# Two edits to the small matmuls of a two-block transformer kernel: scores of both directions added before one product with the values; softmax attention heads taken in pairs on halves of the array

## The reference, cut to what matters

```
scores = einsum('bhnik,bhnjk->bhnij', qe, ke)
scores = jnp.where(mask, scores, 0.0)
o_intra = jnp.einsum('bhnij,bhnjv->bhniv', scores, v)
...
o_inter = jnp.einsum('bhnik,bhnkv->bhniv', q * jnp.exp(b), s_start)
o = (o_intra + o_inter)
...
o_l = o_l + _flip(ol_d, d, 2)
```

```
s = jnp.einsum('bnigrd,bnjgd->bgrnij', qb, kk).astype(f32) * (dh ** -0.5)
s = s - slopes[None, :, :, None, None, None] * dist.astype(f32)[None, None, None, None]
...
m = jnp.maximum(jnp.max(s, axis=-1, keepdims=True), sink)
p = jnp.exp(s - m)
p = p / (jnp.sum(p, axis=-1, keepdims=True) + jnp.exp(sink - m))
out = jnp.einsum('bgrnij,bnjgd->bnigrd', p, vv.astype(f32))
...
y_s = swa @ w_swa_out[l]
```

## Time and profile before

| | |
|---|---|
| median of 3 runs | 909.81 us (908.39 to 911.15) |
| the profiled execution | 909.08 us, of which its span is 907.3 us |
| TensorE busy | 892.5 us of the span |
| TensorE weight loads busy | 808.8 us |
| VectorE busy | 655.4 us |
| ScalarE busy | 492.6 us |
| mean traffic | 177 GB/s |

### The profile page before, as it was taken

The page is one execution under the profiler, slowest core; times in us unless marked ns, Lnnn a source line. Parts: engine busy times, 40 slices in busy tenths (PEclk is TensorE's granted clock), DMA queues, the critical chain, the costliest instruction groups (busy, mean ns, idle before and its releaser), DMA issues.

```text
span 907.3 us, 17399 instructions
## 1 busy us (share of the span) xinstructions
PE 892.5 (98%) x6478; PEld 808.8 (89%) x6478; DVE 655.4 (72%) x1092; ACT 492.6 (54%) x769; POOL 0.2 (0%) x4
## 2 busy tenths in 40 slices
PE   8999999999999999999999999999999999999997
PEld 3578888888899999999999998999998899999996
DVE  3977798888886777766678978876576765555555
ACT  4632576666674655555557444454464664444443
POOL 0000000000000000000000000000000000000000
PEclk9999999999999999999999999999999999999999
DMA  9758844444435355556554643355446366555551
GB/s 339 296 187 284 313 149 140 139 139 139 139 116 202 111 192 194 185 165 201 173 178 139 209 140 123 111 186 182 153 164 210 111 203 208 185 185 185 186 185 47
DMA packets 45583, 160.88 MB, mean 177 GB/s; under 512 B 5216, under 2 KB 6624, under 8 KB 45408
## 3 DMA queue, kind: packets, MB, share of 16 engines
q1 hardware_dynamic: 43488, 156.27, 50.5%
q10 hardware_dynamic: 2048, 3.97, 1.2%
HBM read 159.16 MB, written 1.05 MB: 177 GB/s over the span
## 4 chain that ended last, share of the span: by engine, by line
PE 88%; DVE 4%; DMA 3%; ACT 3%; issue 2%; SPq 0%; DVEq 0%; ACTq 0%
PE bank L429 21%; PE bank L431 21%; PE bank L430 21%; PE bank L495 4%; PE bank L496 4%; PE bank L497 4%; DMA arena<-in_ada 2%; DMA raw<-in_stream 1%; PE bank L1154 1%; DVE arena L1586 1%; ACT w_hi L416 1%; PE bank L1299 1%; PE bank L1279 1%; PE bank L1295 1%; PE bank L1197 1%
## 5 line engine op out<-in xcount | busy, mean ns | idle before, releaser
L423 DVE TENSOR_TENSOR w_lo<-raw,w_hi 128x1024 fp32r<-128x1024 f32 x252 | 304.4, 1223 | 136.0 <-ACT w_hi L416 135.6
L429 PE MATMUL bank<-h_hi,w_hi 128*128 128x256 f32 (+1 forms) x1232 | 369.2, 300 | 2.3 <-DVE w_lo L423 1.4
L430 PE MATMUL bank<-h_lo,w_hi 128*128 128x256 f32 (+1 forms) x1232 | 361.6, 293 | 0.0
L431 PE MATMUL bank<-h_hi,w_lo 128*128 128x256 f32 (+1 forms) x1232 | 361.2, 293 | 0.0
L416 ACT ACTIVATE w_hi<-raw 128x1024 fp32r<-128x1024 f32 x252 | 261.0, 1051 | 134.9 <-PE bank L431 87.5
L429 PEld LDWEIGHTS bank<-h_hi,w_hi 128*128 128x128 f32 x1232 | 231.2, 188 | 12.7 <-issue 2.9
L430 PEld LDWEIGHTS bank<-h_lo,w_hi 128*128 128x128 f32 x1232 | 232.1, 188 | 6.5
L431 PEld LDWEIGHTS bank<-h_hi,w_lo 128*128 128x128 f32 x1232 | 232.5, 189 | 5.9
L429 PE MATMUL bank<-y_hi,w_hi 128*128 128x256 f32 x304 | 86.9, 286 | 0.0
L430 PE MATMUL bank<-y_lo,w_hi 128*128 128x256 f32 x304 | 85.8, 282 | 0.0
L431 PE MATMUL bank<-y_hi,w_lo 128*128 128x256 f32 x304 | 85.3, 281 | 0.0
(11 more groups left out here) (255 smaller groups left out, 1095.1 us busy)
## 6 DMA issues: line engine op xcount, KB each, us to landing
raw<-in_stream SPq DMA_DIRECT2D x252, 512.0 KB, 4.2
arena<-in_ada SPq DMA_DIRECT2D x32, 512.0 KB, 5.1
xres<-in_ada SPq DMA_DIRECT2D x8, 512.0 KB, 3.3
tok<-in_tok SPq DMA_DIRECT2D x3, 512.0 KB, 9.5
con<-in_con ACTq DMA_DIRECT2D x1, 1472.0 KB, 11.2
xres<-in_tok ACTq DMA_DIRECT2D x1, 1024.0 KB, 8.3
out<-arena SPq DMA_DIRECT2D x4, 256.0 KB, 2.1
tok<-in_tok SPq DMA_DIRECT2D x2, 256.0 KB, 11.2
```

The costliest lines, as they stand in the source:

```text
L423: dve.tensor_tensor(w_lo[c.slot][:, :], raw[c.slot][:, :], w_hi[c.slot][:, :].bitcast(F32), ALU.subtract).then_inc(S("split_lo"), 1)
L429: pe.matmul(dst, hi_w, a_hi, start=start, stop=False, skip_group_check=True)
L430: pe.matmul(dst, hi_w, a_lo, start=False, stop=False, skip_group_check=True)
L431: return pe.matmul(dst, lo_w, a_hi, start=False, stop=stop, skip_group_check=True)
```

## The change

**Recurrence.** After the masked copy, DVE adds the two directions' halves of `sc_T` into a new 128 by 256 area `sc_both` (in `wide`), after waiting for its own masked copy. `outputs` waits for this addition, and multiplies `v_cur` with `sc_both` once for each block, instead of twice with `sc_T`.

**Softmax attention.** Step e now handles head `head_of(e)`: 0, 4, 1, 5, 2, 6, 3, 7. Slopes and sinks follow. The scores of steps e and e+1 (e even) are issued together behind tile 10 + 2e, one head on the lower and one on the upper 64 rows, in turn, into banks 5 and 6. The values of steps e-1 and e (e odd) are issued together behind tile 14 + 2e, one head on the lower and one on the upper 64 columns, in turn. DVE copies the results of both heads at once. The rows of `w_swa_out_2` are reordered on the host to match.

```diff
+def head_of(e):
+
+    return 4 * (e % 2) + e // 2
...
+        sc_both = wide[:, 3584:3584 + NB * P]
...
             def probs_copy(e):
                 act.wait_ge(S("p_turned"), e + 1)
                 if e >= 2:
-                    act.wait_ge(S("pv"), e - 1)
+                    act.wait_ge(S("pv"), e // 2)
...
-                pe.wait_ge(S("masked"), h + 1)
+                pe.wait_ge(S("masked"), h * 2 + 2)
                 pe.wait_ge(S("state"), h * 4 + 4)
                 for b in range(NB):
                     dst = o_bank[:, b * P:(b + 1) * P]
-                    for d in range(2):
-                        x = (2 * d + b) * P
-                        pe.matmul(dst, v_cur[:, b * P:b * P + P], sc_T[:, x:x + P], start=d == 0, stop=False,
-                                  skip_group_check=True)
+                    pe.matmul(dst, v_cur[:, b * P:b * P + P], sc_both[:, b * P:b * P + P], start=True, stop=False,
+                              skip_group_check=True)
...
             def swa_scores(e):
-                g, x = e // 4, (e % 4) * T
-                rows = slice(S_DH * g, S_DH * g + S_DH)
+                x = e // 2 * T
                 if e == 0:
                     pe.wait_ge(S("in2_copied"), T_VS)
-                if e >= 2:
-                    pe.wait_ge(S("s_biased"), e - 1)
-                dst = psum[5 + e % 2]
-                pe.matmul(dst[:, 0:P], s_q[rows, x:x + P], s_k[rows, 0:P], start=True, stop=True, skip_group_check=True)
-                pe.matmul(dst[:, P:3 * P], s_q[rows, x + P:x + T], s_k[rows, 0:T], start=True, stop=True,
-                          skip_group_check=True).then_inc(S("s_scores"), 1)
+                else:
+                    pe.wait_ge(S("s_biased"), e)
+                for g in range(2):
+                    rows = slice(S_DH * g, S_DH * g + S_DH)
+                    pe.matmul(psum[5 + g][:, 0:P], s_q[rows, x:x + P], s_k[rows, 0:P], start=True, stop=True,
+                              skip_group_check=True)
+                for g in range(2):
+                    rows = slice(S_DH * g, S_DH * g + S_DH)
+                    pe.matmul(psum[5 + g][:, P:3 * P], s_q[rows, x + P:x + T], s_k[rows, 0:T], start=True, stop=True,
+                              skip_group_check=True).then_inc(S("s_scores"), 1)
...
             def swa_values(e):
-                g, q = e // 4, S_DH * (e % 2)
+                pair = e // 2
                 pe.wait_ge(S("p_T"), e + 1)
-                if e == 0:
+                if pair == 0:
                     pe.wait_ge(S("v2"), 1)
-                if e >= 2:
-                    pe.wait_ge(S("swa"), e - 1)
-                pe.matmul(psum[4][q:q + S_DH, 0:T], s_v[:, S_DH * g:S_DH * g + S_DH], s_pT[e % 2][:, 0:T],
-                          start=True, stop=False, skip_group_check=True)
-                pe.matmul(psum[4][q:q + S_DH, P:T], s_v[:, P + S_DH * g:P + S_DH * g + S_DH], s_pT[e % 2][:, T:3 * P],
-                          start=False, stop=True, skip_group_check=True).then_inc(S("pv"), 1)
+                else:
+                    pe.wait_ge(S("swa"), pair)
+                for g in range(2):
+                    q = S_DH * g
+                    pe.matmul(psum[4][q:q + S_DH, 0:T], s_v[:, q:q + S_DH], s_pT[g][:, 0:T], start=True, stop=False,
+                              skip_group_check=True)
+                for g in range(2):
+                    q = S_DH * g
+                    last = pe.matmul(psum[4][q:q + S_DH, P:T], s_v[:, P + q:P + q + S_DH], s_pT[g][:, T:3 * P], start=False,
+                                     stop=True, skip_group_check=True)
+                last.then_inc(S("pv"), 1)
...
-                for after, step in ((0, swa_scores), (3, turn_probs), (4, swa_values)):
-                    if swa_at(t, after) is not None:
-                        step(swa_at(t, after))
+                if swa_at(t, 0) is not None and swa_at(t, 0) % 2 == 0:
+                    swa_scores(swa_at(t, 0))
+                if swa_at(t, 3) is not None:
+                    turn_probs(swa_at(t, 3))
+                if swa_at(t, 4) is not None and swa_at(t, 4) % 2 == 1:
+                    swa_values(swa_at(t, 4))
...
+                dve.wait_ge(S("masked"), h * 2 + 1)
+                dve.tensor_tensor(sc_both, sc_T[:, 0:NB * P], sc_T[:, NB * P:], ALU.add).then_inc(S("masked"), 1)
...
             def swa_copy(e):
-                q = S_DH * (e % 2)
-                dve.wait_ge(S("pv"), e + 1)
-                dve.tensor_copy(swa[q:q + S_DH, (e // 2) * T:(e // 2 + 1) * T], psum[4][q:q + S_DH, 0:T]).then_inc(S("swa"), 1)
+                pair = e // 2
+                dve.wait_ge(S("pv"), pair + 1)
+                dve.tensor_copy(swa[:, pair * T:(pair + 1) * T], psum[4][:, 0:T]).then_inc(S("swa"), 1)
...
+    swa_out = a["w_swa_out_2"][0].reshape(2, 4, S_DH, D).transpose(1, 0, 2, 3).reshape(512, D)
```

More of the change, by code:

```diff
@@ L1014, in softmax_exp @@
             def softmax_exp(e):
-                p = e % 2
+                p, head = e % 2, head_of(e)
                 act.wait_ge(S("s_neg"), e + 1)
@@ L1022, in softmax_exp @@
                                bias=s_neg[p][:, 1:2], accum_out=s_sum[p][:, 1:2]).then_inc(S("s_exp"), 1)
-                act.activation(s_sink[p], s_neg[p], ACT.Exp, bias=sink[:, e:e + 1]).then_inc(S("s_exp"), 1)
+                act.activation(s_sink[p], s_neg[p], ACT.Exp, bias=sink[:, head:head + 1]).then_inc(S("s_exp"), 1)
             def probs_copy(e):
@@ L1066, in _ @@
                 if swa_at(t, 6) == S_HEADS - 1:
-                    act.wait_ge(S("swa"), S_HEADS)
+                    act.wait_ge(S("swa"), S_HEADS // 2)
                     act.activation(h_hi[:, 8 * T:12 * T], swa, ACT.Copy).then_inc(S("swa_hi"), 1)
@@ L1477, in ret_values @@
                 if r == 0:
-                    pe.wait_ge(S("swa"), S_HEADS)
+                    pe.wait_ge(S("swa"), S_HEADS // 2)
                     pe.wait_ge(S("v_step"), 3)
@@ L2000, in softmax_max @@
                 p = e % 2
-                slope = 2.0 ** (-8.0 / S_HEADS * (e + 1))
+                head = head_of(e)
+                slope = 2.0 ** (-8.0 / S_HEADS * (head + 1))
                 dve.wait_ge(S("s_scores"), e + 1)
@@ L2010, in softmax_max @@
                 dve.wait_ge(S("s_max"), e + 1)
-                dve.tensor_scalar(s_neg[p], s_max[p], -(S_DH ** -0.5), sink_neg[:, e:e + 1], ALU.mult,
+                dve.tensor_scalar(s_neg[p], s_max[p], -(S_DH ** -0.5), sink_neg[:, head:head + 1], ALU.mult,
                                   ALU.min).then_inc(S("s_neg"), 1)
@@ L2078, in _ @@
                     silu(t - 2)
-                for after, step in ((1, softmax_max), (2, softmax_norm), (5, swa_copy)):
+                for after, step in ((1, softmax_max), (2, softmax_norm)):
                     if swa_at(t, after) is not None:
                         step(swa_at(t, after))
+                if swa_at(t, 5) is not None and swa_at(t, 5) % 2 == 1:
+                    swa_copy(swa_at(t, 5))
                 if swa_at(t, 7) == S_HEADS - 1:
@@ L2247 @@
     stream = np.concatenate([v[:1], first[KT:KT + 4], v[1:2], first[KT + 4:], v[2:], heads, _rows(a["hg_w_out"][0]), np.stack(ffn),
[L2248 removed]
+                             in2, _rows(swa_out), _rows(a["w_ret_out_2"][0]), _rows(a["w_out_2"][0]), np.stack(mlp)])
     lb = a["hg_lb_logits"]
```

1 line of the change is left out of this document (removed).

## The result

The changed kernel took 897.44 us in the median of 4 runs (895.85 to 900.37), the kernel before 909.5 us (908.39 to 911.15, 4 runs): a ratio of 0.987, 95% interval 0.984 to 0.9899. It is faster, by more than forecast, and 897.44 lies 0.9 us under the range of 898.3 to 904.6. The profiled execution took 897.38 us with a span of 895.6.

A forecast was written before the change was run, and what follows sets the result against it. PE's matmul program was taken to bound the kernel; 3.6 us from the recurrence plus 5.9 us from attention, 9.5 us off 909.8, gave 900.3 us (50%). The range was 898.3 to 904.6 us.

The forecast's parts named there:

- signs of being wrong: PE waiting for `k_far`, `masked` or a `w_lo` in the recurrence, or attention pair parts taking 1.6 us or more.
- What bounds the kernel: Recurrence and attention: PE is busy throughout, so work taken from its program shortens the run equally while DVE and ACT keep up.
- Recurrence, 3.56 us: In `outputs`, two of eight products go per head: 8 heads x 2 x 0.222 us = 3.56 us less on PE.
- The addition at nothing: Recurrence on DVE: the added sum delays DVE 0.49 us per head, hidden by its idle time, so costed at nothing.
- the margin of 2.84 us ahead of the transposes: Recurrence: `k_far` ends 2.84 us before PE's transposes; even without DVE's idle times this was said to absorb the 0.49 us.
- Attention, changes of shape: Softmax attention: four score and four value parts, with one head of each pair counted, cost 4 x (1.04 + 0.99) = 8.12 us.
- Attention, the second head: Softmax attention: each pair's second head adds 0.05 us for values and 0.20 for scores; 5.9 us saved, bounds 1.6 to 6.9.
- Strict order of passes: Attention rival, 17%: passes start only in program order, each pair part costs 0.22 us more than one head; 901.1 us.
- Only columns overlap: Attention rival, 12%: only column halves overlap, so the scores' second head costs its full 0.66 us; 902.2 us.
- nothing overlaps: Attention rival, 7%: the pairing gives no overlap, only 1.6 us from fewer changes of shape; 904.6 us.
- both drain rivals: Attention, 24 changes of halves: 0.18 us each gives 908.9 us (5%); 0.37 us with unhidden weight load gives 913.5 us (3%).
- DVE takes nothing back: Recurrence rival, 6%, claimed the opposite: the addition's 0.49 us reaches PE in every head, 3.9 us; 904.2 us.

The follow-up runs named there:

- the version with the wait moved: Changed kernel with the wait for `qg` placed behind half of the output projection's first row tile: 898.93 us, ratio 0.9923 to the kernel before.
- the experiments with none, four and nine: Changed kernel with the score addition left out, done four times, or done nine times per head: 900.71, 899.32 and 913.25 us.
- the version head by head: Changed kernel with both products of a pair's first head issued ahead of both of the second: 896.91 us, ratio 0.9901 to the kernel before.
- The second comparison: The changed kernel, unaltered, run again beside the kernel before: 898.77 us against 907.45, ratio 0.9903.

## Why the forecast missed its range, point by point

The mechanism was right, and the sum missed by sizes: 9.5 us forecast, 10.1 us shown by the stages, 12.1 us measured. None of the signs of being wrong that the prediction names came up: the one wait for a `w_lo`, 0.5 us ahead of the loop, is there in the kernel before too.

- **What bounds the kernel: right.** TensorE's busy time fills both stages after the change as before, and what left its program left the time.
- **Recurrence, 3.56 us: right in the loop, mis-sized by 0.37 us in all.** The period went from 22.31 to 21.86 us as forecast, by 0.445. The step that failed is that 8 x 0.445 us all reach the time, with no wait outside the loop. Behind the outputs of head 6 TensorE waits for `qg` of the last head; before the change DVE's product ended at 261.03 + 0.69 = 261.72 us, 0.18 us ahead of the row tile's start at 261.90, and the shortened products brought TensorE there before DVE. The text looked at `k_far` and at the waits inside the loop, and left out the one behind it. 3.2 us were measured, by stages and by the edit alone; the version with the wait moved shows that the wait was for `qg`.
- **The addition at nothing: right**, by the experiments with none, four and nine. The delay of 0.49 us and the shrinking of 0.76 us to 0.06 were forecast; 0.16 are left. One argument beside it was not right: the margin of 2.84 us ahead of the transposes is no cover for every head, as the nine additions show; it can be used once. What covers the addition in every head is DVE's idle time.
- **Attention, changes of shape: right.** 8.12 us with one head of each pair free was a sum of 1.04 and 0.99 us, and the profile after shows exactly these for two heads.
- **Attention, the second head: mis-sized.** I took 0.05 us for values and 0.20 for scores, 1.0 us together, "nearer to nothing than to 0.66". It is 0.01 us or less for both. `chunk_scores` had shown it for columns; that rows behave the same was not in the profile before, and the weights of 128 columns for both heads do not go through one after the other. This is the mis-sized term of the sum: 5.9 us were forecast, the gain is the upper bound of the text, 6.9 us, and the version with both heads on the same rows shows that the side-by-side part of it is real.
- **The rivals.** Strict order of passes is refuted, by the profile after and by the version head by head. "Only columns overlap", "nothing overlaps" and both drain rivals are refuted by the 1.28 us and 1.23 us. DVE takes nothing back in the loop, where the period is 21.86 us. The prediction's sentence that puts strict order's sum at the second rival points at the wrong one: strict order is the first of the list, 901.1 us. Neither came true.
- **The range.** With both sizes right the sum would have been 3.2 + 6.9 = 10.1 us, 899.7 us, inside the range. The measured 12.1 us hold 1.6 us (in the profiled pair) that stand ahead of every edit. The second comparison gave 8.8 us for the same pair of kernels, and 898.77 us, inside the range. The step that failed is the 1.0 us that I allowed for the spread of the medians: three medians of the kernel before lie 3.6 us apart (with a change of chip among them), the first transposes of one and the same kernel up to 0.8 us, and four runs of each side do not tell 10 from 12 us. That the 12.1 us were partly such luck is argued from the spread, not shown for the runs without a profile.

## What to carry to other kernels

If TensorE is the bound and a small matmul uses half the rows or half the columns of the array, a partner on the other half was free here, even when it stood behind it in the program; the change of shape was paid once for both. The operation given to another engine was free up to that engine's idle time in a period, which can be read from the gaps before its waits (one addition cost nothing, eight further ones set the period); but shortening the bounding engine's work eats the same gaps, and the waits outside the loop, where a cover of the loop may be missing, have to be gone through one by one. A gain of 1% needs its stages compared, start of stage to start of stage, before the medians are believed.

## What the hardware showed that I had not expected

- Two pairs of float32 products on different 64-row halves with 128 columns of weights each, into different banks, took the time of one: 1.04 us for both heads with the change of shape, 1.69 us on the same rows. Their weight loads did not queue: the four of the first products lie within 0.30 us in the profile after, within 0.52 us on the same rows.
- The order in the program did not hold passes back: with four passes of the first head ahead of the second head's first, the part took 0.01 us more.
- The same instructions reached the recurrence between 114.1 and 119.2 us in twelve profiles, 5 us of a run of 900. The latest of them had a wait of 2.95 us behind a late transfer and after it a granted clock of 0.54 between 98 and 100 us; five of the twelve had such a fall, and took some 2 us longer from there to the transposes.
